# Where the PE queue turns h for the experts: behind the shared expert's products, or directly behind the router's scores

## The chip, the cores and the metric

One core of a Trainium2 chip runs the whole program. The metric is the device time of one execution in microseconds; three executions of the kernel before are shown, and a fourth was taken with the hardware profiler. Every engine works through its own instructions in their order and waits on semaphores for the others; data moves by DMA, issued from the SyncE queue (SP) and, for a few transfers, from GpSimd's (POOL).

## The reference

Two layers of a first block, then two layers of a second block, over 256 tokens of width 1024, all in float32. Each layer of the first block ends in a mixture of experts; this is the part that is touched.

```python
def moe_ffn(u, w_router, b_router, w1, w3, w2, ws1, ws3, ws2):
    ...
    scores = jax.nn.sigmoid((xf @ w_router).astype(jnp.float32))
    biased = scores + b_router.astype(jnp.float32)
    ...
    _, idx = lax.top_k(jnp.where(expert_mask, biased, NEG_INF), TOP_K)
    w = jnp.take_along_axis(scores, idx, axis=-1)
    w = w / (jnp.sum(w, axis=-1, keepdims=True) + 1e-20) * ROUTED_SCALE
    ...
    routed = jax.ops.segment_sum(y.reshape(n_slots, D), slot_tok, num_segments=T + 1)[:T]
    shared = swiglu(xf, ws1, ws3, ws2)
    return (routed + shared).reshape(B, S, D)
```

Eight of 64 experts are chosen for each token; each expert is `(silu(x @ w1) * (x @ w3)) @ w2` with 256 hidden columns, and the shared expert is the same over all tokens.

## The kernel before

The order of the work is written by hand: one generator for each engine records that engine's instructions, and semaphores tie them together. `K.bank(key, only=n)` hands out PSUM bank n and makes PE wait until the last reader of that bank, named by its key, is done.

At the start of a layer's mixture of experts, h (the normalised input) lies in SBUF by features, 8 blocks of 128 features by 256 tokens, in `K.h`, the first half of `hT`. PE then does, in this order (`pe_moe_start`): the router's logits (L1664), the first 8 products of the shared expert's gate half (L271, called from L1671), the logits turned to tokens in bank 6 (L1676), 24 more of the shared expert's products (L271), 16 transposes of h in four groups of four (L1685) into banks 6, 4, 5 and 6, and the products that count the tokens ahead of each one in its expert's list (L271 again, "places" below), for which it waits for `("chosen", l)`. ACT makes the sigmoid of the scores (L1755), two silus of the shared expert's halves (L1759), and copies the four groups of turned h (L1763) to `K.hx`, the second half of `hT`. DVE goes from the scores through the choice of the experts (L1776 to L1823), multiplies the two halves of the shared expert (L1826, j = 0 and 1), and then makes the matrix `K.below` (L1828), with which it signals `chosen`:

```python
    for j in range(2):
        ve.wait_ge(*(yield ("shared_silu", l, j)))
        ve.tensor_tensor(K.gs[:, j, :], K.ss[:, j, :], K.ps["shared_up", l, j][:, 256:512],
                         ALU.mult).then_inc(*K.dve("shared_g", l, j))
    ve.tensor_tensor(K.below, K.ones, C(K, "from_s"), ALU.subtract).then_inc(*K.dve("chosen", l))
```

Three things wait for the turned h. POOL writes it to DRAM (L2266), from where the rows of passes 1 to 4 are fetched by indirect DMAs (L2280) once the experts are ranked. The selection of pass 0 multiplies it (L1893). And SP's next load, the down weights of an expert, goes into the first half of `hT` over h itself (L528), so it waits until PE has read h for the last time; all later loads of expert weights stand behind it in SP's queue. After the places come the shared expert's down products (L1702), the first slots (L1878) and the passes over the experts (up products L1919, down products L1951, scatter L1964), whose weights come into buffers that PE's passes before have to release.

Of the kernel before, what the change touches and what calls it, by code (L numbers as in the profile page):

```python
# [11 lines left out]
ACT = mybir.ActivationFunctionType  # L12
AX = mybir.AxisListType.X

P = 128
# [253 lines left out]
def products(te, o, pairs, first=True, last=True, lax=False):  # L269
    for i, (l, r) in enumerate(pairs):  # L270
        ins = te.matmul(o, l, r, start=(first and i == 0), stop=(last and i == len(pairs) - 1), skip_group_check=lax)  # L271
    return ins
# [76 lines left out]
def k_major(flat, n, k=8):  # L349
    return flat[:, 0:k * n].rearrange("p (k n) -> p k n", k=k)  # L350
# [26 lines left out]
def ring_plan(K):  # L377
# [25 lines left out]
    def views(name, kind, u):  # L403
        if kind == "wide":
            return K.wbuf[u][0].rearrange("p m n -> p (m n)") if name == "up" else K.wbuf[u][1]
        return {"x": K.gate_a.rearrange("p k t -> p (k t)"), "h": K.hT[:, 0:2048], "consts": K.cst_place}[kind]

    def experts(l):


        where = K.where[l]
        wide = [("proj_ps", l, 2, 7), ("mod", *later_parts(l)[-1])]
        first = {"wide": wide, "x": [("merged", l, 0, 7)], "h": [("h_turned", l, 1, 1)],
                 "consts": [("used", "down", 0, K.where[0]["consts"][1])] if l else []}
        for p, of in enumerate(PASS):
            if l == 1 and p == CTX_AT - 1:
                K.plan(("ctx",), 1, [(lambda f: f.rearrange("p (i d) -> p i d", i=2), I["ctx_2"][0].rearrange(
                    "(i p) d -> p i d", p=P))], (K.hT[:, 0:2048], [("used", "down", 1, where["ctx"][1])]))
            for name in ("up", "down"):
                for r, _ in of:  # L420
                    (kind, u), before = where[name, r]
                    if name == "up":
                        parts = [(lambda f: f[:, 0:UNIT], ("w1", 8)), (lambda f: f[:, UNIT:2 * UNIT], ("w3", 8))]
                    else:
                        parts = [(lambda f: f[:, 0:UNIT], ("w2", 2))]
                    if kind in ("slot", "half", "last"):
                        place = kind, u
                    else:
                        place = views(name, kind, u), [("used", before[0], l, before[1])] if before else first[kind]
                    K.plan((name, l, r), len(parts), parts, place)  # L430
# [234 lines left out]
def later_parts(l):  # L665

    if l == 0:
        return [("mod", 1, j) for j in range(5)]
    return [("mod2", q, j) for q in range(2) for j in range(3)]
# [248 lines left out]
def act_norm(K, tag, c0, n, h, shift, sq, r, before, table=True):  # L918
    yield from act_norm_sum(K, tag, c0, n, sq, r, before, table)
    yield from act_norm_shift(K, tag, n, h, shift)  # L920


def pe_norm(K, tag, n, sq):
    b = yield from K.bank(("rstd", tag))
    for k in range(8):
        if k % 2 == 0:
            K.te.wait_ge(*(yield ("sq", tag, k)))
        ins = K.te.matmul(b[:, 0:n], K.ones, sq[:, k, :], start=(k == 0), stop=(k == 7))
    ins.then_inc(*K.pe("norm_sum", tag, ps=b))
# [717 lines left out]
def weights_up(K, l, e):  # L1647
    return K.flat["up", l, e][:, 0:2 * UNIT].rearrange("p (m k f) -> p m k f", m=2, k=8)
# [7 lines left out]
def pe_moe_start(K, l):  # L1656
    te, h = K.te, K.h
    yield from pe_norm(K, ("ffn", l), 256, K.sq8)
    w = k_major(K.flat["router", l], EXPERTS)
    rb = yield from K.bank(("logits", l), only=7)  # L1660
    te.wait_ge(*(yield ("ring", "router", l)))
    for kk in range(8):
        te.wait_ge(*(yield ("h", ("ffn", l), kk, 0)))
        ins = te.matmul(rb[0:64, 0:256], w[:, kk, :], h[:, kk, :], start=(kk == 0), stop=(kk == 7))  # L1664
    ins.then_inc(*K.pe("logits_ps", l, ps=rb))
    K.pe.also("used", "router", l)
    w = weights_up(K, l, EXPERTS)
    te.wait_ge(*(yield ("ring", "up", l, EXPERTS)))
    for j, bank in enumerate((4, 5)):
        b = yield from K.bank(("shared_g", l, j), only=bank)  # L1670
        products(te, b[:, 0:256], [(w[:, 0, kk, j * P:(j + 1) * P], h[:, kk, :]) for kk in range(8)])  # L1671
        if j == 0:
            rb = yield from K.bank(("scores", l), only=6)
            te.wait_ge(*(yield ("logits", l)))
            for i in range(2):
                ins = te.transpose(rb[:, i * 64:(i + 1) * 64], K.t_b[0:64, i * P:(i + 1) * P], K.ident[0:64, 0:64])  # L1676
            ins.then_inc(*K.pe("logits_turned", l, ps=rb))
        products(te, b[:, 256:512], [(w[:, 1, kk, j * P:(j + 1) * P], h[:, kk, :])
                                     for kk in range(8)]).then_inc(*K.pe("shared_up", l, j, ps=b))
    K.pe.also("used", "up", l, EXPERTS)  # L1680
    for i in range(2):
        for q in range(2):
            b = yield from K.bank(("hx", l, i, q), only=(6, 4, 5)[(2 * i + q) % 3])
            for k in range(4):
                ins = te.transpose(b[:, k * P:(k + 1) * P], h[:, 4 * q + k, i * P:(i + 1) * P], K.ident)  # L1685
            ins.then_inc(*K.pe("h_turned", l, i, q, ps=b))

    b = yield from K.bank(("places", l), ("counted", l), only=7)
    te.wait_ge(*(yield ("chosen", l)))
    products(te, b[:, 0:64], [(K.below, K.rep[:, 0, :])])  # L1690
    products(te, b[:, 64:128], [(K.ones, K.rep[:, 0, :]), (K.below, K.rep[:, 1, :])])
    products(te, b[:, 192:256], [(K.ones, K.rep[:, i, :]) for i in range(2)])
    products(te, b[0:64, 128:129], [(K.rep[:, i, :], K.ones[:, 0:1])
                                    for i in range(2)]).then_inc(*K.pe("ranks", l, ps=b))
    w2 = k_major(K.flat["down", l, EXPERTS], D, 2)
    te.wait_ge(*(yield ("ring", "down", l, EXPERTS)))
    te.wait_ge(*(yield ("shared_g", l, 1)))
    for n in range(4):
        i, q = divmod(n, 2)
        yb = yield from K.bank(only=n)  # L1700
        for j in range(2):
            ins = te.matmul(yb[:, :], K.gs[:, j, i * P:(i + 1) * P], w2[:, j, q * 512:(q + 1) * 512], start=(j == 0),  # L1702
                            stop=False, skip_group_check=True)
        if n == 1:
            yield from pe_first_slots(K, l)
            yield from pe_selected(K, l, 0)
            yield from pe_lists_turned(K, l)
    ins.then_inc(*K.pe("shared_down", l))
    K.pe.also("used", "down", l, EXPERTS)
    yield from pe_lists_ranked(K, l)  # L1710


def pe_first_slots(K, l):
    K.rot, K.turn = [4, 5, 6, 7], 0
    b = yield from K.bank(("slot", l, 0), ("slot", l, 1))
    for p in range(2):
        ins = yield from pe_slots(K, l, p, b, 2 * p)
    ins.then_inc(*K.pe("slot_ps", l, 0))
    K.pe.also("slot_ps", l, 1)
# [28 lines left out]
def act_moe_start(K, l):  # L1748
    ac = K.ac
    yield from act_norm(K, ("ffn", l), 256, 256, K.h, [K.mods[l][:, 0, 3, :]], K.sq8, K.r1,  # L1750
                        lambda k: (("mix_out", l, k), ("mix_out", l, k + 1)))
    ac.wait_ge(*(yield ("logits_ps", l)))
    ac.activation(K.t_b[0:64, :], K.ps["logits_ps", l][0:64, 0:256], ACT.Copy).then_inc(*K.act("logits", l))
    ac.wait_ge(*(yield ("logits_turned", l)))
    ac.activation(K.sc, K.ps["logits_turned", l][:, 0:128].rearrange("p (i e) -> p i e", i=2),  # L1755
                  ACT.Sigmoid).then_inc(*K.act("scores", l))
    for j in range(2):
        ac.wait_ge(*(yield ("shared_up", l, j)))
        ac.activation(K.ss[:, j, :], K.ps["shared_up", l, j][:, 0:256], ACT.Silu).then_inc(*K.act("shared_silu", l, j))  # L1759
    for i in range(2):  # L1760
        for q in range(2):
            ac.wait_ge(*(yield ("h_turned", l, i, q)))
            ac.activation(K.hx[:, i, q * 512:(q + 1) * 512], K.ps["h_turned", l, i, q][:, :],  # L1763
                          ACT.Copy).then_inc(*K.act("hx", l, i, q))


def dve_moe_start(K, l):
# [1872 lines left out]
```

## Time and profile before

| what | value |
|---|---|
| median of three runs | 2583.08 us (2575.36 to 2583.17) |
| the profiled execution | 2581.89 us |
| its span | 2580.6 us |
| PE busy | 2468.2 us, 96% of the span |
| DVE busy | 732.2 us, 28% |
| ACT busy | 509.4 us, 20% |
| bytes moved | 634.55 MB, mean 246 GB/s |
| mean granted clock of TensorE | 0.988 |

The time of the profiled execution is its span and 1.3 us around it. The touched stretch occurs twice, once in each layer: from 408 to 426 us and from 1285 to 1303 us.

### The profile page before, as it was taken

The page shows a single profiled execution, that of the slowest core. Times are in us where ns is not written, and L with a number is a line of the kernel's source. Part 1 is how long each engine was busy: PE and PEld are TensorE (multiplying, and loading weights), DVE is VectorE, ACT ScalarE, POOL GpSimd, SP SyncE. Part 2 cuts the span into 40 slices and gives each one's busy share as a digit, 9 for nine tenths or more (in the row PEclk, how much of TensorE's full clock was granted, in tenths as well). Part 3 has the DMA queues.
Part 4 walks back from the last instruction along what each step waited for, and adds up shares of the span by engine and source line. Part 5 has one row for each costly group of instructions (what it writes and reads, how often), then busy time and mean ns, then how long its engine had stood idle before and what let it go on. Part 6 is the DMA issues. An engine that isn't in the chain of part 4 may idle for free.

```text
span 2580.6 us, 30644 instructions
## 1 busy us (share of the span) xinstructions
PE 2468.2 (96%) x12219; PEld 1510.3 (59%) x12219; DVE 732.2 (28%) x1998; ACT 509.4 (20%) x1098; POOL 111.4 (4%) x152
## 2 busy tenths in 40 slices
PE   7998999999999999989999999998999999999998
PEld 4765896444544467658853454444546677664764
DVE  0484213222111117631231221111331322211164
ACT  2224202000000021341110000012222121211253
POOL 4000000000000001010000000000000000001110
PEclk9999999999999999999999999999999999999999
DMA  9867654999999974386579999999206211210210
GB/s 347 286 229 250 242 213 179 414 420 400 420 420 421 398 265 144 116 314 218 228 292 420 395 421 419 420 418 342 71 1 212 66 33 66 82 57 19 96 66 17
DMA packets 176891, 634.55 MB, mean 246 GB/s; under 512 B 13041, under 2 KB 47129, under 8 KB 127073
## 3 DMA queue, kind: packets, MB, share of 16 engines
q1 hardware_dynamic: 171008, 621.74, 61.9%
q0 software_dynamic: 5296, 10.71, 1.2%
q8 instruction: 101, 1.65, 0.3%
q14 instruction: 54, 0.43, 0.1%
q10 hardware_dynamic: 432, 0.01, 0.0%
HBM read 630.28 MB, written 3.52 MB: 246 GB/s over the span
## 4 chain that ended last, share of the span: by engine, by line
PE 84%; DMA 9%; DVE 3%; ACT 2%; issue 1%; SPq 1%; POOL 0%; ACTq 0%; DVEq 0%
PE ps L271 41%; PE ps L1919 12%; PE ps L1951 6%; PE ps L1964 6%; PE ps L1893 5%; DMA ar<-in_w 5%; PE ps L1529 2%; DMA ring<-in_w_mod 2%; PE ps L635 2%; PE ps L2608 2%; PE ps L1010 1%; PE ps L3198 1%; DVE ar L1138 1%; SPq L528 1%; DMA ring<-in_w 1%
## 5 line engine op out<-in xcount | busy, mean ns | idle before, releaser
L271 PE MATMUL ps<-hT,ring 128*128 128x256 f32 (+2 forms) x2480 | 641.0, 416 | 3.4 <-ACT xT L1482 3.4
L271 PEld LDWEIGHTS ps<-hT,ring 128*128 128x128 f32 (+1 forms) x2480 | 465.6, 190 | 174.0 <-issue 115.1
L1919 PE MATMUL ps<-ring,ar 128*32 128x512 f32 (+2 forms) x1328 | 340.3, 605 | 23.5 <-DMA ar<-in_w 23.5
L1919 PE MATMUL ps<-ar 128*64 128x512 f32 (+2 forms) x720 | 284.1, 613 | 4.8 <-DMA ring<-in_w 3.6
L1919 PEld LDWEIGHTS ps<-ring,ar 128*32 128x32 f32 (+2 forms) x1328 | 102.3, 126 | 222.5 <-issue 218.5
L1964 PE MATMUL ps<-ar 128*128 128x512 f32 x400 | 184.8, 604 | 0.0
L1893 PEld LDWEIGHTS ps<-ar,hT 128*128 128x128 f32 x1344 | 154.8, 192 | 12.0 <-issue 11.7
L1893 PE MATMUL ps<-ar,hT 128*128 128x128 f32 x1344 | 161.2, 276 | 0.0
L271 PE MATMUL ps<-ring,hT 128*128 128x256 f32 (+1 forms) x640 | 156.5, 402 | 0.0
L271 PEld LDWEIGHTS ps<-ring,hT 128*128 128x128 f32 x640 | 120.9, 190 | 40.1 <-issue 25.9
L2235 DVE TENSOR_TENSOR ar<-ar,ps 128x256 f32<-128x256 f32 x50 | 21.1, 421 | 428.0 <-ACT ar L2084 418.1
L271 PE MATMUL ps<-ring,ar 128*128 128x512 f32 x320 | 138.4, 593 | 0.0
L1964 PEld LDWEIGHTS ps<-ar 128*128 128x128 f32 x400 | 71.8, 188 | 111.6 <-issue 110.7
L1951 PE MATMUL ps<-ar 128*64 128x512 f32 (+1 forms) x272 | 125.2, 602 | 0.0
L2084 ACT ACTIVATE ar<-ps 128x256 f32<-128x256 f32 x50 | 19.2, 384 | 499.3 <-PE ps L1919 499.3
L1919 PEld LDWEIGHTS ps<-ar 128*64 128x64 f32 (+2 forms) x720 | 78.1, 127 | 44.5 <-issue 42.3
L271 PEld LDWEIGHTS ps<-ring,ar 128*128 128x128 f32 x320 | 60.5, 190 | 74.5 <-issue 74.5
L271 PE MATMUL ps<-ar,ring 128*128 128x256 f32 (+1 forms) x416 | 99.0, 395 | 1.3 <-DVE ar L1301 0.7
L1138 DVE SCALAR_TENSOR_TENSOR ar<-ar,wdw 128x256 f32<-128x256 f32 x240 | 98.0, 483 | 0.0
L1951 PE MATMUL ps<-ring,ar 128*32 128x512 f32 (+2 forms) x256 | 92.3, 602 | 1.6 <-DMA cst<-in_w 1.6
L271 PEld LDWEIGHTS ps<-ar,ring 128*128 128x128 f32 x416 | 78.7, 190 | 18.5 <-issue 8.4
L1951 PE MATMUL ps<-xT,ar 128*64 128x512 f32 (+1 forms) x184 | 85.1, 606 | 0.0
(441 smaller groups left out, 2560.6 us busy)
## 6 DMA issues: line engine op xcount, KB each, us to landing
ring<-in_w SPq DMA_DIRECT2D x198, 1024.0 KB, 19.9
ar<-in_w SPq DMA_DIRECT2D x124, 1024.0 KB, 14.2
ring<-in_w_mod SPq DMA_DIRECT2D x36, 2048.0 KB, 13.4
ring<-in_w_in SPq DMA_DIRECT2D x28, 2048.0 KB, 16.8
ring<-in_ab_w_in SPq DMA_DIRECT2D x28, 1024.0 KB, 11.8
xT<-in_w SPq DMA_DIRECT2D x23, 1024.0 KB, 15.3
cst<-in_w SPq DMA_DIRECT2D x21, 1024.0 KB, 18.9
hT<-in_w SPq DMA_DIRECT2D x18, 1024.0 KB, 22.7
```

What stands on the lines that cost most here:

```text
L271: ins = te.matmul(o, l, r, start=(first and i == 0), stop=(last and i == len(pairs) - 1), skip_group_check=lax)
L528: sp.dma_start(dst, src).then_inc(landed[k], 16)
L635: ins = te.matmul(b[32 * t:32 * t + 32, :], col(2 * t + s), w[:, 2 * t + s, :], start=(s == 0), stop=(s == 1))
L1010: ins = te.matmul(b[:, :], h[:, kk, i * P:(i + 1) * P], w[0][:, kk, :], start=(kk == 0), stop=(kk == 7))
L1138: ins = ve.scalar_tensor_tensor(K.acc[:, c, :], K.hpad[:, c, k:k + 256], tap, K.acc[:, c, :], ALU.mult, ALU.add)
L1529: ins = te.matmul(b[:, 0:256], w[kk // 4][:, kk % 4, k::8], K.merged[:, kk, :], start=(kk == 0), stop=(kk == 7))
L1893: ins = te.matmul(b[:, (k % 4) * P:(k % 4 + 1) * P], K.hx[:, i, k * P:(k + 1) * P], K.f_s[p % 2][:, i, :], start=(i == 0), stop=(i == 1))
L1919: ins = te.matmul(b[cols, :], K.x_b[:, kk, cols], weights_up(K, l, r)[:, :, kk, :], start=(kk == 0), stop=(kk == 7))
L1951: ins = te.matmul(b[cols, :], K.t_b[:, j * P + cols.start:j * P + cols.stop], weights_down(K, l, r, j, q), start=(j == 0), stop=(j == 1))
L1964: ins = te.matmul(K.banks[2 * i + q][:, :], K.wT[p % 2][:, i * P:(i + 1) * P], K.o_b[:, q * 512:(q + 1) * 512], start=False, stop=False, s ...
L2608: ins = te.matmul(b[:, cols], w[:, kk, c * P:(c + 1) * P], h[:, kk, cols], start=(kk == 0), stop=(kk == 7))
L3198: ins = te.matmul(b[:, 0:256], w[:, kk, (n % 2) * P:(n % 2 + 1) * P], hx[:, kk, :], start=(kk == 0), stop=(kk == 7))
```

## The change

In PE's order the four groups of transposes move from behind the shared expert's products to directly behind the turned scores, inside the loop over j, and they get banks 0 to 3 in place of 6, 4, 5, 6. ACT's four copies move ahead of its two silus. SP's load over h waits for the last of the shared expert's products in place of the last transpose.

```diff
@@ ring_plan: experts
-        first = {"wide": wide, "x": [("merged", l, 0, 7)], "h": [("h_turned", l, 1, 1)],
+        first = {"wide": wide, "x": [("merged", l, 0, 7)], "h": [("shared_up", l, 1)],
@@ pe_moe_start
             ins.then_inc(*K.pe("logits_turned", l, ps=rb))
+            for i in range(2):
+                for q in range(2):
+                    hb = yield from K.bank(("hx", l, i, q), only=2 * i + q)
+                    for k in range(4):
+                        ins = te.transpose(hb[:, k * P:(k + 1) * P], h[:, 4 * q + k, i * P:(i + 1) * P], K.ident)
+                    ins.then_inc(*K.pe("h_turned", l, i, q, ps=hb))
         products(te, b[:, 256:512], [(w[:, 1, kk, j * P:(j + 1) * P], h[:, kk, :])
                                      for kk in range(8)]).then_inc(*K.pe("shared_up", l, j, ps=b))
     K.pe.also("used", "up", l, EXPERTS)
-    for i in range(2):
-        for q in range(2):
-            b = yield from K.bank(("hx", l, i, q), only=(6, 4, 5)[(2 * i + q) % 3])
-            for k in range(4):
-                ins = te.transpose(b[:, k * P:(k + 1) * P], h[:, 4 * q + k, i * P:(i + 1) * P], K.ident)
-            ins.then_inc(*K.pe("h_turned", l, i, q, ps=b))
@@ act_moe_start
-    for j in range(2):
-        ac.wait_ge(*(yield ("shared_up", l, j)))
-        ac.activation(K.ss[:, j, :], K.ps["shared_up", l, j][:, 0:256], ACT.Silu).then_inc(*K.act("shared_silu", l, j))
     for i in range(2):
         for q in range(2):
             ac.wait_ge(*(yield ("h_turned", l, i, q)))
             ac.activation(K.hx[:, i, q * 512:(q + 1) * 512], K.ps["h_turned", l, i, q][:, :],
                           ACT.Copy).then_inc(*K.act("hx", l, i, q))
+    for j in range(2):
+        ac.wait_ge(*(yield ("shared_up", l, j)))
+        ac.activation(K.ss[:, j, :], K.ps["shared_up", l, j][:, 0:256], ACT.Silu).then_inc(*K.act("shared_silu", l, j))
```

PE's queue at this place in layer 0 (layer 1 has the same), `hT` being h and `ring` the shared expert's weights; each row is a run of equal instructions, lines with - are the kernel before, lines with + the changed one, and the last row is the first of the places:

```order
 L1676 MATMUL ps6<-cst,ar 128x64 x2
+L1682 MATMUL ps0<-cst,hT 128x128 x4
+L1682 MATMUL ps1<-cst,hT 128x128 x4
+L1682 MATMUL ps2<-cst,hT 128x128 x4
+L1682 MATMUL ps3<-cst,hT 128x128 x4
 L271 MATMUL ps4<-hT,ring 128x256 x8
 L271 MATMUL ps5<-hT,ring 128x256 x16
-L1685 MATMUL ps6<-cst,hT 128x128 x4
-L1685 MATMUL ps4<-cst,hT 128x128 x4
-L1685 MATMUL ps5<-cst,hT 128x128 x4
-L1685 MATMUL ps6<-cst,hT 128x128 x4
 L271 MATMUL ps7<-ar 128x64
```

The number of instructions is the same. Before, the transposes stood between the last product and the places; now nothing stands there.

ACT's queue at the same place, from the sigmoid of the scores on (L1759 and L1764 are the silus of the shared expert's two halves, L1763 and L1760 the copies of turned h):

```order
 L1755 ACT_TABLE_LOAD
 L1755 ACTIVATE ar<-ps 128x128
-L1759 ACT_TABLE_LOAD
-L1759 ACTIVATE ar<-ps 128x256 x2
-L1763 ACTIVATE hT<-ps 128x512 x4
+L1760 ACTIVATE hT<-ps 128x512 x4
+L1764 ACT_TABLE_LOAD
+L1764 ACTIVATE ar<-ps 128x256 x2
```

The copies and the silus have changed places; no table load is added. The queues of DVE, POOL and SP hold the same instructions in the same order.

## Rows read from the trace of the kernel before

**Rows 1.** The page: span, and the engines' busy time.

```profile
span 2580.6 us, 30644 instructions
PE 2468.2 (96%) x12219; PEld 1510.3 (59%) x12219; DVE 732.2 (28%) x1998; ACT 509.4 (20%) x1098; POOL 111.4 (4%) x152
```

**Rows 2.** The page: the chain that ended last, by engine.

```profile
PE 84%; DMA 9%; DVE 3%; ACT 2%; issue 1%; SPq 1%; POOL 0%; ACTq 0%; DVEq 0%
```

**Rows 3.** Timeline, layer 0, 408 to 423 us: start, length, instruction, idle before it.

```profile
408.24 0.33 PE L1676 MATMUL ps<-cst,ar 64*128 64x64 f32 x2
408.50 10.63 PE L271 MATMUL ps<-hT,ring 128*128 128x256 f32 x48
408.90 1.28 ACT L1759 ACT_TABLE_LOAD   x1
...
418.28 0.41 DVE L1826 TENSOR_TENSOR ar<-ar,ps 128x256 f32<-128x256 f32 x1
...
418.97 2.19 PE L1685 MATMUL ps<-cst,hT 128*128 128x128 f32 x16
419.17 0.38 ACT L1759 ACTIVATE ar<-ps 128x256 f32<-128x256 f32 x1 [6.52 <-PE ps L271]
419.58 0.42 DVE L1826 TENSOR_TENSOR ar<-ar,ps 128x256 f32<-128x256 f32 x1 [0.89 <-ACT ar L1759]
419.60 2.24 ACT L1763 ACTIVATE hT<-ps 128x512 f32<-128x512 f32 x4
419.92 0.29 DVE L1828 TENSOR_TENSOR ar<-cst 128x128 f32<-128x128 f32 x1
420.06 0.86 PEld L1685 LDWEIGHTS ps<-cst,hT 128*128 128x128 f32 x8 [0.29 <-DVE ar L1826]
420.88 0.30 PEld L271 LDWEIGHTS ps<-ar 128*128 128x128 f32 x2
...
422.43 0.73 POOL L2266 DMA_DIRECT2D hx_rows<-hT  x1 [133.44 <-ACT hT L1763]
```

**Rows 4.** Timeline, layer 1: the same products, and the first load of the places.

```profile
1285.72 10.63 PE L271 MATMUL ps<-hT,ring 128*128 128x256 f32 x48
...
1298.10 0.30 PEld L271 LDWEIGHTS ps<-ar 128*128 128x128 f32 x2
```

**Rows 5.** Timeline of SP's queue, 396 to 450 us.

```profile
421.18 0.33 SPq L528 DMA_DIRECT2D hT<-in_w  x1
421.56 2.77 SPq L528 DMA_DIRECT2D ring<-in_w  x5
449.04 0.33 SPq L528 DMA_DIRECT2D ar<-in_w  x1
```

**Rows 6.** Windows: stretch, length, busy time of each engine, PEclk, DMA share, GB/s.

```profile
404.00:421.00 17.00, 16.94 (x87) 14.21 (x85) 9.37 (x56) 5.33 (x9) 0.00 (x0) 1.00 0.02 9
...
426.00:436.00 10.00, 10.00 (x75) 7.54 (x76) 1.64 (x8) 1.19 (x2) 0.00 (x0) 1.00 1.01 407
...
442.00:449.00 7.00, 6.22 (x42) 3.04 (x40) 2.74 (x10) 1.58 (x3) 1.02 (x1) 1.00 0.12 26
449.00:506.00 57.00, 57.00 (x306) 21.56 (x306) 11.71 (x39) 4.74 (x9) 1.99 (x2) 1.00 0.99 401
...
524.00:534.00 10.00, 10.00 (x66) 2.95 (x67) 0.00 (x0) 0.18 (x1) 0.00 (x0) 0.73 1.02 421
```

**Rows 7.** DMA issues from 420 to 437 us: KB each, us to landing.

```profile
hx_rows<-hT POOLq DMA_DIRECT2D x1, 1024.0 KB, 13.4
```

**Rows 8.** Waits of SP's queue from 425 to 450 us: total, times, longest.

```profile
SPq L528 <- PE ps L1951: 24.7, 1, 24.7
```

**Rows 9.** The chain that ended last, in order of time: stalls for weights and passes behind.

```profile
507.32 16.55 DMA ar<-in_w
524.00 9.75 PE ps L1919 x61
...
674.15 7.10 PE ps L1919 x32
```

## The prediction

> **What bounds the kernel now.** I read the page's engine line and its chain first. PE is busy for 2468.2 of 2580.6 us [rows 1], and the chain that ended last runs over PE for 84% of the span and over DMA for 9% [rows 2]. So a moved PE instruction gains nothing by being moved: PE has to do it in any case. It gains only if it fills a stretch in which PE would stand still, and it loses if it leaves such a stretch behind. The question is where PE stands still around the shared expert, and the timeline of that place answers it [rows 3].
>
> There PE works through the shared expert's last 48 recorded products (24 in the program, each recorded twice) from 408.50 without a gap until 408.50 + 10.63 = 419.13 us. DVE's whole choice of the experts lies beneath them: its first product of the shared halves, which stands behind the choice in DVE's order, starts at 418.28. So when PE comes to its last product, the choice is as good as made. What is still missing for the places is a short chain that starts only with that last product: the second silu at 419.17 (0.38 us), the second product on DVE at 419.58 (0.42 us), and behind it in DVE's order the matrix `below` from 419.92 to 420.21, which carries the signal `chosen` [rows 3]. PE doesn't notice most of this chain, because it turns h meanwhile: 16 transposes from 418.97 on, 2.19 us with one gap of 0.29 us, in which the third group waited for bank 5 and so for the second product on DVE. The first load of the places starts at 420.88, 0.67 us after `chosen`. Layer 1 repeats this to the hundredth: the products end at 1285.72 + 10.63 = 1296.35, and the places start at 1298.10 [rows 4].
>
> **The change, part by part.**
>
> The transposes, in front. 16 of them now stand behind the turned scores. Eight loads of transposes took 0.86 us where nothing stopped them [rows 3], so 16 take 1.72 us, and everything behind them, the 48 recorded products, ends that much later: 419.13 + 1.72 = 420.85. This cannot be hidden, as PE had no idle time between 408.24 and 419.13. The bound above is the 2.19 us of all 16 with their gap. Banks 0 to 3 are no new wait: their last readers belong to the norm and to the mixer's output, all ahead of the logits, and the turned scores at 408.24 have waited for the logits' copy.
>
> The transposes, behind. What stood between the end of the products and the first load of the places was 420.88 − 419.13 = 1.75 us, and it goes.
>
> The chain, uncovered. In its place PE now waits for silu, product and `below`. Nothing of them gets shorter: the silu started 0.04 us after the end of the products, `below` ended at 420.21, which is 1.08 us after it, and PE took about 0.06 us from DVE's end to its next load (product done at 420.00, load at 420.06). That is 1.14 us [rows 3].
>
> So per layer 1.72 − 1.75 + 1.14 = **+1.11 us**: the first load of the places moves from 420.88 to about 421.99. A first matmul stood some 0.1 us behind its load when PE came to it without a wait, and closer after one, which I take off in half: +1.05 us. The bound above is 2.19 − 1.75 + 1.14 = 1.58. The bound below is 0, where the uncovered chain costs no more than what the transposes filled; a real gain on PE alone is not to be had beyond the one gap of 0.29 us.
>
> ACT. The four copies (2.24 us) now start when the first group is turned, about 409.0, and end by 411.4; the table load of 1.28 us follows and is over by 412.7. The first silu needs the first third of the 48 recorded products, which now end at about 408.50 + 1.72 + 10.63 / 3 = 413.8, so nothing waits for ACT. If it did, the cover is large: that silu's result is first used by DVE at 418.28. The second silu finds ACT idle, as before. ACT costs nothing.
>
> DVE. Same order. Its choice still ends at 418.3, now 2.5 us ahead of PE's last product, where before it was 0.8 us ahead. It waits longer for the second silu and is not the bound.
>
> POOL and the write of the turned rows. The write of 1 MB was issued at 422.43 and took 13.4 us to land [rows 3, 7], as it shared the DMA engines with six expert loads: from 426 to 436 us they were full, at 407 GB/s [rows 6]. It will now be issued at about 411.5, in a stretch in which DMA moves 9 GB/s [rows 6], and land long before the loads start. 1.05 MB at 407 GB/s is 2.6 us of DMA time taken out of the busy stretch. I cost this gain at nothing. The six loads of this burst run out on their own: from 442 to 449 us the DMA engines are 12% busy [rows 6], because SP waits 24.7 us for PE's down products of pass 0 and issues again only at 449.04 [rows 5, 8]. What lands 2.6 us earlier has only a longer rest before it is used. The fetch of pass 1 needs the ranking, which comes after the places and so about 1.05 us later.
>
> The Trainium skill (DMA: Bandwidth & Descriptors, Anatomy of one DMA) gives about 2.0 us and bytes / 436e3 for one DMA from this queue, which for 1.05 MB makes an estimate of 4.4 us against the 13.4 us here. By the page alone the change would bring 9 us for whatever waits on this write; in this trace, nothing on PE waits for it.
>
> SP. Its load over h was issued at 421.18, behind the last transpose [rows 5]. It now waits for the last product, ending at 420.85, and goes about 0.3 us earlier, as do the five behind it. The same rest at 442 us swallows this. The next issue, at 449.04, hangs on PE and moves by 1.05 us.
>
> From there to the end. The passes wait for each other on both sides: the loads wait until PE releases buffers, and from 449 on DMA is 99% busy [rows 6]; PE waits for loads at 507 us and later [rows 9]. Both the start of the load stream and PE's passes hang on the places, so both shift by the same 1.05 us, and so do the stalls. No slack in the later stage can swallow it, since the stage's whole start is late.
>
> Sum: 2 layers × 1.05 = +2.1 us, from 2581.89 in the profiled execution to 2584.0. That execution is 1.2 us under the median of the runs, so for the median I add the same to 2583.08: **2585.2 us**, +0.08%. By the bounds 0 and 1.58 per layer it is 2583.1 to 2586.2. About 0.3% (7.7 us) is what a measurement of this kernel can tell from no change, and its three runs alone spread over 7.8 us. My forecast is therefore "same", a little on the slow side. Chance 0.73.
>
> **The rivals.**
>
> *The write out of the load stream counts.* If the burst at 421 us were already part of the stretch that DMA bounds, then the stage would start 0.3 us earlier and lose 2.6 us of traffic, and PE's delay would be swallowed in its first stall: −2.9 us per layer, 2583.1 − 5.8 = 2577.3 us. For it speaks the full DMA share from 426 to 436; against it the rest from 442 to 449, and SP's wait for PE. Chance 0.08.
>
> *The move does nothing.* The last products end later but PE finds `chosen` ready, because something on PE's way is shorter than I read, such as the transposes pipelining better between matmuls of another shape: 0 per layer, 2583.1 us. Against it is that `below` hangs on the second silu, and this on PE's last product, in both orders. Chance 0.07.
>
> *The stalls for weights reach further down.* This is the one on the slow side. Behind the stall at 507 us the granted clock of TensorE was 0.73 from 524 to 534 us [rows 6], a mean over its two levels, 1.2 and 2.4 GHz, and the pass there took 9.75 us; the one at 674, also behind a wait for weights, took 7.10 [rows 9]. A stall that now ends in time and then does not costs the difference, 2.65 us. With the 2.1 us of the forecast, it takes three more such falls in the two layers to pass the bound of 7.7 us: 10.1 us, about 2593 us. For it speaks that PE and DMA hand each other their delays through the whole stage; against it that both begin shifted by the same amount. Chance 0.07. The mirror image, fewer falls because loads come relatively earlier (the 2.6 us of traffic, if part of it survives), would give −8 us, 2575 us: chance 0.05.
>
> **How the numbers follow.** The time is that of the likeliest case, 2585.2. Its own range, with the runs' spread of 7.8 us, goes down to 2578 and up to 2589; the first and second rival lie inside or at its lower edge. The range 2577 to 2590 leaves out the last rival and its mirror, 0.12 together, and some scatter. Faster by over 0.3% is the mirror (0.05), slower the third rival (0.07), the rest is the same: 0.88.
>
> **What the changed profile would show.** Right: the 16 transposes directly behind the turned scores, in about 1.7 us and without a wait; the products ending 1.7 us later; PE idle for about 1.1 us ahead of the places, released by DVE's `below`; the first load of the places near 422.0 if the stretch ahead is unchanged; the write of h issued near 411.5 and landed in some 4 to 6 us; SP's load over h about 0.3 us earlier, its next issue after the burst about 1 us later; the stalls for weights as many and as long as before. Wrong: the places no later than before (second rival); SP's issue after the burst no longer released by PE, or fewer stalls (first rival and mirror); more passes of 9 us and above behind stalls (third). My sum is wrong where the transposes between products cost more than 2.2 us, or where PE's new idle stretch has another releaser than DVE.

## The result and the profile after

Over 20 runs of each kernel, taken side by side, the changed kernel has a median of 2585.35 us (2578.2 to 2590.82) and the kernel before one of 2579.22 us (2574.37 to 2586.77). The ratio is 1.0022, with a 95% interval of [1.0015, 1.003]: the change costs 0.22% or 5.7 us, between 3.9 and 7.7. That is within the 0.3% that the prediction calls "the same", and it is a real loss, more than twice the 2.1 us of the forecast. The three runs of before that stood at the time of the prediction had a median 3.9 us above that of the 20; that 2585.2 and 2585.35 agree so closely is owed to this, and is no merit of the sum.

The whole spans of two profiled executions can't show the loss: that of the changed kernel, 2579.9 us, is shorter than that of before [rows 1]. So I read a stretch whose two ends mean the same in both kernels, from PE's first router product (L1664) to its first up product of pass 0 (L1919). Before, it takes 34.90 us in each layer. The timeline of the kernel before, layer 0 (the second line is the first of the places, the third the shared expert's down products):

```profile
401.02 3.64 PE L1664 MATMUL ps<-hT,ring 128*64 128x256 f32 x16 [2.24 <-ACT hT L914]
...
420.99 0.33 PE L271 MATMUL ps<-ar 128*128 128x64 f32 x2
...
422.47 3.70 PE L1702 MATMUL ps<-ring,ar 128*128 128x512 f32 x8
...
435.92 7.10 PE L1919 MATMUL ps<-ar 128*64 128x512 f32 x32
```

The timeline of the changed kernel, layer 0 (start, length, instruction, idle time before it), corresponds to [rows 3]:

```profile
398.58 3.64 PE L1664 MATMUL ps<-hT,ring 128*64 128x256 f32 x16 [2.24 <-ACT hT L914]
...
406.07 1.73 PEld L1682 LDWEIGHTS ps<-cst,hT 128*128 128x128 f32 x16
...
406.76 2.06 ACT L1760 ACTIVATE hT<-ps 128x512 f32<-128x512 f32 x4 [0.31 <-PE ps L1682]
...
407.87 10.53 PE L271 MATMUL ps<-hT,ring 128*128 128x256 f32 x48
...
409.42 0.73 POOL L2266 DMA_DIRECT2D hx_rows<-hT  x1 [122.89 <-ACT hT L1760]
...
415.95 0.41 DVE L1826 TENSOR_TENSOR ar<-ar,ps 128x256 f32<-128x256 f32 x1
...
418.44 0.38 ACT L1764 ACTIVATE ar<-ps 128x256 f32<-128x256 f32 x1 [6.52 <-PE ps L271]
...
419.19 0.29 DVE L1828 TENSOR_TENSOR ar<-cst 128x128 f32<-128x128 f32 x1
...
419.62 0.41 PE L271 MATMUL ps<-ar 128*128 128x64 f32 x2 [1.22 <-DVE ar L1828]
...
421.30 5.21 PE L1702 MATMUL ps<-ring,ar 128*128 128x512 f32 x8
...
436.26 7.10 PE L1919 MATMUL ps<-ar 128*64 128x512 f32 x32
```

The transposes stand ahead and take 1.73 us. The products end at 407.87 + 10.53 = 418.40. The silu, the product and `below` follow, and PE idles 1.22 us, released by `below`. Its first matmul of the places stands 419.62 − 398.58 = 21.04 us behind the start of the stretch, where before it stood at 19.97: 1.07 us late. Up to here this is the forecast. Then comes what the forecast doesn't have: the 8 recorded down products of the shared expert (L1702) take 5.21 us, and 3.70 before. The stretch ends at 37.68 us, 2.78 late. In layer 1 it is the same, 37.69 us. The windows of that place in the changed kernel show what is slow (the columns are those of [rows 6], the last four POOL, PEclk, DMA share, GB/s):

```profile
418.40:419.60 1.20, 0.00 (x0) 0.01 (x1) 0.62 (x2) 0.38 (x1) 0.00 (x0) 1.00 0.33 55
419.60:421.30 1.70, 1.68 (x14) 1.62 (x15) 0.00 (x0) 0.00 (x0) 0.00 (x0) 0.90 0.71 270
421.30:423.30 2.00, 2.00 (x4) 0.97 (x4) 1.82 (x11) 0.00 (x0) 0.00 (x0) 0.50 1.01 426
423.30:425.30 2.00, 2.00 (x5) 0.92 (x4) 1.05 (x6) 0.00 (x0) 0.00 (x0) 0.73 1.03 434
425.30:427.30 2.00, 2.00 (x21) 1.03 (x20) 0.16 (x3) 0.00 (x0) 0.00 (x0) 1.00 1.00 422
```

The granted clock is still 1.00 during the idle stretch, 0.90 on average over the small matmuls of the places, 0.50 (1.2 GHz) over the first down products, and back at 1.00 (2.4 GHz) from 425.3 on. In the kernel before, the windows from 416 to 429 us show 1.00 throughout; these two hold the places and the first down products:

```profile
421.00:423.00 2.00, 2.00 (x17) 1.68 (x16) 0.39 (x2) 0.84 (x2) 0.57 (x1) 1.00 0.38 78
423.00:425.00 2.00, 2.00 (x6) 0.95 (x5) 1.91 (x13) 0.00 (x0) 0.16 (x1) 1.00 0.93 377
```

The other steps went as foreseen. The write of turned h (DMA issues of the changed kernel, 406 to 421 us) landed after 4.4 us in place of 13.4 [rows 7], and SP's queue now shows, in place of [rows 5]:

```profile
hx_rows<-hT POOLq DMA_DIRECT2D x1, 1024.0 KB, 4.4
```

```profile
418.43 0.33 SPq L528 DMA_DIRECT2D hT<-in_w  x1
418.80 2.70 SPq L528 DMA_DIRECT2D ring<-in_w  x5
449.38 0.33 SPq L528 DMA_DIRECT2D ar<-in_w  x1
```

Measured from L1664, the load over h went out at 19.85 us (before: 421.18 − 401.02 = 20.16), 0.3 us earlier, and the first load after the burst at 50.80 us (before: 48.02), later by the same 2.78 us as the stretch. The load stream waited for PE and was shifted with it.

### The profile page after: what moved, and what is told of

It reads as the page before. It is cut to its first block, busy times and chain, and to the rows that moved or that the text cites. A ratio compares the mean times of both kernels' runs of the same rounds, so it can differ in the third digit from the quotient of the medians.

```text
span 2579.9 us, 30646 instructions
## 1 busy us (share of the span) xinstructions
PE 2469.1 (96%) x12219; PEld 1512.2 (59%) x12219; DVE 734.1 (28%) x1998; ACT 509.2 (20%) x1098; POOL 109.8 (4%) x152
## 4 chain that ended last, share of the span: by engine, by line
PE 84%; DMA 8%; DVE 3%; ACT 2%; issue 1%; SPq 1%; POOL 0%; ACTq 0%; DVEq 0%
PE ps L271 41%; PE ps L1919 12%; PE ps L1951 6%; PE ps L1964 6%; PE ps L1893 5%; DMA ar<-in_w 4%; PE ps L1529 2%; PE ps L635 2%; PE ps L2608 2%; DMA ring<-in_w 1%; PE ps L1010 1%; PE ps L3198 1%; DVE ar L1138 1%; SPq L528 1%; DMA ring<-in_w_in 1%
## 5 line engine op out<-in xcount | busy, mean ns | idle before, releaser
L1919 PE MATMUL ps<-ring,ar 128*32 128x512 f32 (+2 forms) x1328 | 341.8, 605 | 24.4 <-DMA ar<-in_w 24.2
L1919 PE MATMUL ps<-ar 128*64 128x512 f32 (+2 forms) x720 | 285.6, 614 | 3.6 <-DMA ring<-in_w 3.6
L1919 PEld LDWEIGHTS ps<-ring,ar 128*32 128x32 f32 (+2 forms) x1328 | 103.1, 126 | 223.4 <-issue 219.6
L1919 PEld LDWEIGHTS ps<-ar 128*64 128x64 f32 (+2 forms) x720 | 78.6, 128 | 44.4 <-issue 44.2
```

The lines of the kernel that those rows point to most:

```text
L1919: ins = te.matmul(b[cols, :], K.x_b[:, kk, cols], weights_up(K, l, r)[:, :, kk, :], start=(kk == 0), stop=(kk == 7))
```

## The experiments

Each is told by the stretch from L1664 to L1919, in layer 0 and layer 1, and by the ratio of whole runs to the kernel before with its 95% interval (9 to 12 runs, against 17 to 35 of the kernel before taken beside them). "Idle" is PE's idle time ahead of the places. An edit that adds lines moves the line numbers behind it: in filler, L1831 is `below` and L1705 the down products where L1828 and L1702 were.

**Theories.** A: PE's idle stretch ahead of the places (1.1 us) is one half of the loss, and a fall of the clock that it causes is the other. B: the down products are slow for a reason that has nothing to do with the idle stretch, the expert loads beside them or the waits on banks 0 to 3 that they now carry. C, formed after the first batch: the fall is a matter of chance. D: the write of turned h, taken out of the load stream, is worth time that the loss hides.

**below_first: the move stays, the wait goes.** On the changed kernel, DVE makes `below` ahead of the two products:

```diff
+    ve.tensor_tensor(K.below, K.ones, C(K, "from_s"), ALU.subtract).then_inc(*K.dve("chosen", l))
     for j in range(2):
         ve.wait_ge(*(yield ("shared_silu", l, j)))
         ve.tensor_tensor(K.gs[:, j, :], K.ss[:, j, :], K.ps["shared_up", l, j][:, 256:512],
                          ALU.mult).then_inc(*K.dve("shared_g", l, j))
-    ve.tensor_tensor(K.below, K.ones, C(K, "from_s"), ALU.subtract).then_inc(*K.dve("chosen", l))
```

> The changed kernel with one DVE instruction moved: the matrix below, which carries the signal chosen, is made ahead of the two products of the shared expert's halves, so the places no longer wait for the second silu. Times are per layer from the first router product (L1664) to the first up product of pass 0 (L1919): 34.9 us before the change, 37.7 changed. Theory A (idle stretch, then a fall of the clock): PE has no idle stretch ahead of the places, the granted clock stays 1.00, the shared down products (8 recorded) take 3.7 us and not 5.2, and the stretch takes 34.5 to 34.9 us; the whole is 5 to 6.5 us faster than the changed kernel, at or up to 0.8 us below the kernel before. Theory B (the down products are slow for another reason: the expert loads that run beside them, or the waits for banks 0 to 3 that they now carry): the idle stretch goes, 1.2 us, but they still take about 5.2 us, and the stretch takes about 36.2 us.

Measured: 34.57 and 34.58 us, ratio 1.0001 [0.9988, 1.0014]. The timeline of below_first, layer 0:

```profile
413.15 10.53 PE L271 MATMUL ps<-hT,ring 128*128 128x256 f32 x48
...
423.51 0.33 PE L271 MATMUL ps<-ar 128*128 128x64 f32 x2
...
424.99 3.70 PE L1702 MATMUL ps<-ring,ar 128*128 128x512 f32 x8
...
438.44 7.10 PE L1919 MATMUL ps<-ar 128*64 128x512 f32 x32
```

The places follow the products without an idle stretch, and the down products are back at 3.70 us, although they carry the same waits on banks 0 to 3 and run beside the same loads. Theory B falls; the repeats of the changed kernel below, with both sorts of down products at the same waits and loads, settle it. The whole runs speak too: the interval ends below that of the changed kernel, [1.0015, 1.003]. The move of the transposes as such costs nothing; what costs is that `chosen` hung on the second silu, which the transposes had hidden.

**filler: the wait stays, PE is kept at work.** On the changed kernel, ahead of the places (the two products are extra work that nobody reads):

```diff
+    fill = yield from K.bank(only=6)
+    te.wait_ge(*(yield ("hx", l, 1, 1)))
+    products(te, fill[:, 0:256], [(K.ident, K.hx[:, 0, 0:256])] * 2).then_inc(*K.pe())
     b = yield from K.bank(("places", l), ("counted", l), only=7)
```

> The changed kernel with two more products (4 recorded, 0.89 us, of the identity with turned h, into bank 6, read by nobody) between the last of the shared expert's products and the places. The wait for chosen stays. Theory A: PE's idle stretch shrinks from 1.2 to about 0.3 us, the places start at the same time as in the changed kernel, the clock stays at 1.00, the 8 recorded down products take 3.7 us, and the stretch from L1664 to L1919 takes about 36.0 us, 1.5 to 1.7 less than changed: 3 us faster than changed in all. Theory B: nothing changes but the idle share, 37.7 us and 5.2 us.

Measured: 35.98 and 35.98 us, ratio 1.0009 [0.9998, 1.002], 2.3 us over the kernel before. The timeline of filler, layer 0:

```profile
420.71 1.03 PE L271 MATMUL ps<-hT,cst 128*128 128x256 f32 x4
...
422.01 0.43 PE L271 MATMUL ps<-ar 128*128 128x64 f32 x2 [0.27 <-DVE ar L1831]
...
423.59 3.70 PE L1705 MATMUL ps<-ring,ar 128*128 128x512 f32 x8
```

The places are as late as in the changed kernel (20.95 us behind L1664), but with 0.27 us of idle time ahead of them in place of 1.22 the down products take 3.70 us. The two halves of the loss are apart now: 1.08 us is the wait, 1.70 the clock. Against the first profile of the changed kernel, useless work on PE shortened the stretch. Two occurrences alone don't show that it kept the clock up, as the changed kernel too has occurrences without a fall (below); the count at the end of this section carries that reading.

**filler1: one product in place of two.** The edit of filler without `* 2`.

> The changed kernel with one filling product (2 recorded, 0.44 us) in place of two: PE idles about 0.7 to 0.8 us ahead of the places. The places start when they did in the changed kernel, 1.1 us late. Theory A1 (the length of the idle stretch decides): as in the run with 0.75 us of idle time behind the transposes, no fall, down products 3.7 us, stretch 36.0 us, 2 us over the kernel before. Theory A2 (what stands ahead of the idle stretch decides, products in place of transposes): the clock falls, 5.2 us, stretch 37.5 us, 5 us over.

Measured: 0.70 us idle in both layers, down products 3.70 us, stretch 35.97 and 35.98, ratio 1.001 [1.0001, 1.002]. No fall behind 0.70 us, as A1 has it, though two occurrences alone leave room for chance.

**half: half of the transposes early.** Groups 0 and 1 behind the scores, groups 2 and 3 behind the products. ACT's copies are split in the same way, and SP's load over h waits for the last transpose again (neither is shown):

```diff
-            for i in range(2):
+            for i in range(1):
                 for q in range(2):
                     hb = yield from K.bank(("hx", l, i, q), only=2 * i + q)
...
     K.pe.also("used", "up", l, EXPERTS)
+    for q in range(2):
+        hb = yield from K.bank(("hx", l, 1, q), only=2 + q)
+        for k in range(4):
+            ins = te.transpose(hb[:, k * P:(k + 1) * P], h[:, 4 * q + k, P:2 * P], K.ident)
+        ins.then_inc(*K.pe("h_turned", l, 1, q, ps=hb))
```

> Only the two groups of the first 128 tokens are turned early (8 transposes), the other two stay behind the products, all in banks 0 to 3; ACT's copies are split in the same way. Theory A: the products end 0.86 us later than before, the remaining 8 transposes cover 0.86 of the 1.14 us of silu, product and below, so PE idles about 0.3 us, the clock stays at 1.00, and the stretch from L1664 to L1919 takes 35.1 to 35.2 us, 0.25 us more than before: 0.5 us slower than before in all, not to be told from it. Theory B: the down products still take longer than 3.7 us, and the stretch is over 36 us.

Measured: 35.17 and 35.17 us, idle 0.35, down products 3.70, ratio 1.0004 [0.9992, 1.0016]. The working of the prediction (transposes in front, transposes behind, chain uncovered) gives this intermediate point to a few hundredths.

**delay and delay7: the idle stretch without the move.** On the kernel before, DVE makes `below` five (or seven) times more before the one that signals:

```diff
+    for _ in range(5):
+        ve.tensor_tensor(K.below, K.ones, C(K, "from_s"), ALU.subtract).then_inc(*K.dve())
+        ve.wait_ge(*own())
     ve.tensor_tensor(K.below, K.ones, C(K, "from_s"), ALU.subtract).then_inc(*K.dve("chosen", l))
```

> The kernel before (transposes behind the products) with DVE making the matrix below five times more, each after the one ahead of it, before the one that signals chosen: 5 x 0.32 = 1.6 us, nothing else moved. PE finds chosen late by about 1.0 us, as in the changed kernel, but directly behind transposes, not behind products. Theory A: 0.9 to 1.1 us of idle time ahead of the places, then the clock falls to 1.2 GHz, the down products take about 5.2 us, and the stretch from L1664 to L1919 takes 37.3 to 37.6 us, 5 us slower than before in all. Theory B: only the idle time is added, the down products stay at 3.7 us, 35.9 us: 2 us slower in all.

> The kernel before with seven extra copies of below in place of five, so chosen comes 2 x 0.33 us later and PE idles about 1.4 us directly behind the transposes, slightly more than in the changed kernel behind the products. Theory A1 (length decides): the clock falls at the down products, 5.2 us, stretch 34.9 + 1.7 + 1.5 = 38.1 us, 6.4 us over the kernel before in all. Theory A2 (what stands ahead decides): no fall, 3.7 us, stretch 36.6 us, 3.4 us over.

Measured for delay: 0.75 us of idle time, down products 3.70 us in both layers; ratio 1.0003 [0.9992, 1.0014]. The fall that I expected at the down products did not come. It came elsewhere: the stretch took 35.92 us in layer 1, but 37.51 in layer 0, and the timeline of delay, layer 0, has it in the router's products, behind the 2.2 us for which PE always waits for the norm, and the window that follows the timeline here, also of layer 0, shows a granted clock of 0.55:

```profile
400.76 5.24 PE L1664 MATMUL ps<-hT,ring 128*64 128x256 f32 x16 [2.23 <-ACT hT L914]
...
423.24 0.43 PE L271 MATMUL ps<-ar 128*128 128x64 f32 x2 [0.75 <-DVE ar L1831]
...
424.82 3.70 PE L1702 MATMUL ps<-ring,ar 128*128 128x512 f32 x8
```

```profile
400.40:402.40 2.00, 1.64 (x4) 0.98 (x5) 2.00 (x7) 2.00 (x6) 0.00 (x0) 0.55 0.98 414
```

Measured for delay7: 1.40 us of idle time in both layers, 38.28 and 36.57 us, down products 5.40 and 3.70; ratio 1.0027 [1.0015, 1.0039]. The windows of the down products in delay7, layer 0 and then layer 1:

```profile
421.50:424.50 3.00, 3.00 (x5) 1.29 (x5) 2.74 (x16) 0.00 (x0) 0.00 (x0) 0.54 0.99 352
1300.00:1303.70 3.70, 3.70 (x11) 1.50 (x10) 2.87 (x16) 0.00 (x0) 0.00 (x0) 1.00 1.00 355
```

The same idle stretch behind the same transposes made the clock fall in one layer and not in the other. So an idle stretch without any early transposes can cost the second half too. The changed order is not needed for a fall, and neither A1 nor A2, as I had put them, holds.

**after_again, after_third, after_fourth: the changed kernel once more.** No edit; more profiles, to count.

> The changed kernel once more, for a second profile of it and beside the others of this call. Theory A (the idle stretch ahead of the places makes the clock fall there in nearly every execution): in both layers PE idles 1.2 us, the 8 recorded down products take about 5.2 us, the stretch from L1664 to L1919 takes 37.7 us, and the whole is 5 to 6 us over the kernel before. Theory C (whether the clock falls there is a matter of chance): one or both layers show 3.7 us and 36.2 us, and the median lies 2.5 to 5 us over.

> The changed kernel, one more profile, to count at how many of the occurrences the clock falls behind the idle stretch of 1.22 us: 3 of 4 up to now. Theory C (chance, with a fall in more than half): 1 or 2 of the two layers show down products of 5.2 us and a stretch of 37.7 us, the others 3.7 and 36.0. Theory A would have 2 of 2.

> As the run ahead of it: the changed kernel, one more profile, two more occurrences. Theory C: 1 or 2 falls. Theory A: 2.

Measured: 36.04 and 37.67 us for the first, 37.72 and 36.04 for the second, 36.04 and 37.74 for the third; the first has ratio 1.0019 [1.001, 1.0028] from 11 runs. Both sorts stand in one execution, here the windows of after_third, first layer 0 and then layer 1, each the idle stretch, the places and the down products:

```profile
419.10:420.30 1.20, 0.05 (x1) 0.00 (x0) 0.62 (x2) 0.38 (x1) 0.00 (x0) 1.00 0.52 61
420.30:421.90 1.60, 1.52 (x14) 1.49 (x14) 0.00 (x0) 0.00 (x0) 0.00 (x0) 1.00 0.65 256
421.90:424.90 3.00, 3.00 (x6) 1.43 (x6) 2.69 (x16) 0.00 (x0) 0.00 (x0) 0.51 0.99 415
1296.90:1298.10 1.20, 0.06 (x1) 0.00 (x0) 0.62 (x2) 0.38 (x1) 0.00 (x0) 1.00 0.45 61
1298.10:1299.70 1.60, 1.51 (x14) 1.48 (x14) 0.00 (x0) 0.00 (x0) 0.00 (x0) 1.00 0.63 225
1299.70:1303.30 3.60, 3.60 (x10) 1.46 (x9) 2.87 (x16) 0.00 (x0) 0.00 (x0) 1.00 1.02 423
```

The same instructions, the same idle stretch, and a clock of 0.51 once and 1.00 once. Theory C holds, theory A in its strict form does not.

**late_write: the write of turned h held back.** On the changed kernel:

```diff
             gp.wait_ge(*(yield ("hx", l, i, q)))
+    gp.wait_ge(*(yield ("places", l)))
```

> The changed kernel with the write of turned h to DRAM held back until DVE has the places, which puts it again beside the six expert loads, where it was before the change. Theory A: nothing on PE waits for it, so pass 1 and all later stalls stay where they are, and the time is that of the changed kernel within 0.1%. Theory D (taking this write out of the load stream was worth its 1.05 MB, so the change hid a gain of 2.6 us per layer): about 5 us slower than the changed kernel, about 11 over the kernel before.

Measured: ratio 1.002 [1.0009, 1.0031], as the changed kernel has, not 0.4%; stretch 36.04 and 37.73 us. The write landed after 13.8 us, and in layer 0 the fetch of pass 1 now did wait for it:

```profile
439.35 1.11 POOL L2281 DMA_INDIRECT ar<-hx_rows,ar  x1 [13.95 <-DMA hx_rows<-hT]
```

but PE did not: its transposes of the fetched rows (L1906) follow the turned products (L1935) in the timeline of late_write, PE, as they did before:

```profile
444.97 0.51 PE L1935 MATMUL ps<-cst,ar 128*128 128x128 f32 x2 [0.78 <-DVE ar L2235]
445.31 1.04 PE L1906 MATMUL ps<-cst,ar 128*128 128x128 f32 x8
```

They start 8.45 us behind the first up product of pass 0 (L1919), as in the kernel before and in the changed one. Theory D falls: its 11 us would be a ratio of 1.0043, above the interval. Early or late, the freed megabyte was worth nothing that these runs can tell.

**banks: only the banks.** The kernel before with banks 0 to 3:

```diff
-            b = yield from K.bank(("hx", l, i, q), only=(6, 4, 5)[(2 * i + q) % 3])
+            b = yield from K.bank(("hx", l, i, q), only=2 * i + q)
```

> The kernel before with the transposes left behind the products; only their banks change, from 6, 4, 5, 6 to 0, 1, 2, 3, as in the changed kernel. Theory A: the 0.29 us in which the third group waited for bank 5 goes, chosen is ready when PE comes to the places, nothing idles, and the stretch from L1664 to L1919 takes 34.5 to 34.6 us, 0.3 us less than before: 0.7 us in all, which the times of whole runs can't tell from zero. Rival: the gap only moves to the places, where PE then waits for chosen, 34.8 to 34.9 us.

Measured: places 19.69 us behind L1664 in layer 0 (19.97 before), stretch 34.62 us; in layer 1 the clock fell behind the norm (router's products 5.33 us, granted clock 0.53 from 1277.0 to 1279.3 us), which made it 36.31. Ratio 1.0008 [0.9999, 1.0017], so no gain can be shown in whole runs, and the 0.6 us for two layers that the stretch of layer 0 promises stays below what they tell.

**before_second: a control.**

> The kernel before, a second profile of it, as a control: no idle stretch over 0.3 us between the scores and the down products, so no fall there in either layer, 3.7 us and 34.9 us. Behind the norm's 2.2 us of idle time the router's products may be slow in one of the layers (5.2 in place of 3.6 us), as in one layer of one earlier run.

Measured: 34.90 and 34.90 us, router's products 3.64 and down products 3.70 in both layers, no fall.

**The count.** With an idle stretch of 1.22 us ahead of the places (the changed kernel four times, late_write once, two layers each) the down products were slow in 6 of 10 occurrences; with 1.40 us (delay7) in 1 of 2; with at most 0.76 us or none (before, before_second, below_first, filler, filler1, half, delay, banks) in 0 of 16. Behind the norm's idle stretch of 2.2 us, which all 14 profiles have twice, the router's products were slow in 2 of 28.

So it is 7 of 12 behind 1.22 us and more, and 0 of 16 behind less. If the length had no part in it, all seven falls would land among those 12 about once in 1500 times, an estimate that takes the occurrences as independent. It is softer than it looks: below_first, filler, half and delay, 8 of the 16, were profiled together on one chip, with none of the kernels of 1.22 us among them. Without them it is 7 of 12 against 0 of 8, about once in 100.

## Why the prediction was right or wrong

- *The transposes in front*: 1.72 us foreseen, 1.73 measured. Right.
- *The transposes behind and the chain uncovered*: the first load of the places 1.11 us late, measured 1.15 (419.59 − 398.58 = 21.01 against 420.88 − 401.02 = 19.86); the first matmul 1.07 late. Right, and half hits the same working at its other point.
- *ACT, DVE and banks cost nothing*: right. The copies took 2.06 us and the second silu found ACT idle (6.52 us).
- *The write of h and SP's 0.3 us are worth nothing*: right for the write, shown by late_write; for the 0.3 us no run separates them. The write took 13.4 us beside six loads and 4.4 us alone, and nothing on PE waited for it either time. The estimate of 4.4 us from the Trainium skill (DMA: Bandwidth & Descriptors, Anatomy of one DMA) agrees with this trace for the write alone.
- *From there to the end everything shifts by the same amount*: right as far as it was seen. The first load after the burst shifted by 2.78 us with PE. The long stage between the layers (L1919 of layer 0 to L1664 of layer 1) took 842.3 and 842.1 us in the two profiles of before, and 839.4, 837.4, 840.1 and 840.3 in the four of the changed kernel: nothing added. All four are shorter, though, by 1.8 to 4.9 us. The stage scatters by more than this over all 14 profiles, from 837.4 (after_again) to 845.2 us (filler1), so these profiles neither show a gain there nor can confirm the shift to 1 us.
- *The sum of 1.05 us per layer*: this is the step that failed, as a term left out. I had looked for a fall of the clock only behind the long stalls for weights, as the rival on the slow side, and not behind the idle stretch that my own sum made. I didn't ask what the 1.1 us do to the matmuls that follow. They took 1.64 us longer (37.68 − 36.04) in 6 of 10 occurrences, 1.0 us on average, which makes 2 × (1.14 + 1.0) = 4.3 us, inside the measured interval of 3.9 to 7.7 and of 2.6 to 7.2 in the repeat. With a fall in every occurrence it would be 5.6 us. The time of whole runs can't tell these two apart; the profiles can, and speak for about half. What decides whether the clock falls stays open. That the remaining 1.4 us up to 5.7 is scatter is argued, not shown: no run locates it.
- The rival on the slow side named the right mechanism at the wrong place: no more stalls for weights were needed. In the stage between the layers the chain that ended last has two passes of L1919 over 8 us (8.45 to 9.86 us, where others take about 7) in each of the two profiles of before and of the four of the changed kernel.

A version that beats both was looked for in banks and below_first. Both shorten the stretch to 34.6 us, 0.3 below before, and neither can be told from the kernel before in whole runs.

## What to carry to other kernels

Work that PE does between its last product and the first matmul that waits for what ACT and DVE make of that product is a cover: before moving it, write down the chain it hides (here silu, product, one small matrix, 1.1 us) and first move the signal off that chain, as below_first does with one DVE instruction. When a change leaves a new idle stretch on PE, price it twice, once as its length (here 1.14 us) and once as the chance that what comes behind runs at half the clock (here 1.64 us in 6 of 10). A difference of 0.2% shows in whole runs only after many of them, but in one profile when it is read between two instructions that both kernels share. Where chance has a part, one profile misleads: the first of the changed kernel had a fall in both layers, the three repeats in one layer each.

## What the runs showed of the hardware that was not expected

An idle stretch of 1.22 us on PE, followed by 1.6 us of small matmuls (14 recorded, 64 columns or one), let the granted clock fall to 0.50 in 6 of 10 occurrences, while 2.2 us of idle time with products of 256 columns behind it did so in 2 of 28. So the length of the idle stretch alone does not tell whether the clock falls; the work around it or something that changes from execution to execution has a part in it. The changed kernel shows that the latter has one: the same instructions behind the same idle stretch fell in one layer and not in the other. Whether the work has one too, no run here separates: no kernel put such products directly behind the 1.22 us. In no profile of the changed kernel did the clock fall during the idle stretch itself; it fell after PE was at work again. A fall, when it came, cost 1.6 to 1.7 us at either place.
